# Other unread products behind two norms: f32 products of ones become fp32r products of stored tiles

## The reference, cut to what matters

```
# layer 0, x and ctx alike
x = x + gate1 * x_mix
x = x + gate2 * swiglu(modulate(rms_norm(x, norm_ffn[0]), shift2, scale2), w_gate_up[0], w_down[0])
# layer 1
h = modulate(rms_norm(x, norm_mix[1]), shift1, scale1)
q, k, v, hy, g = split(h @ w_in[1])
...
y = xf * rsqrt(mean(xf * xf) + EPS)      # rms_norm
```

## Time and profile before

| | us |
|---|---|
| median of 3 runs | 2101.53 |
| lowest, highest | 2100.41, 2101.59 |
| span of the profiled execution, first to last instruction | 2097.6 |
| TensorE busy (matmuls) | 1903.2, 91% |
| TensorE weight loads | 1550.1, 74% |
| VectorE busy | 1133.1, 54% |
| ScalarE busy | 892.0, 43% |

### The profile page before, as it was taken

The page is one execution under the profiler, slowest core; times in us unless marked ns, Lnnn a source line. Parts: engine busy times, 40 slices in busy tenths (PEclk is TensorE's granted clock), DMA queues, the critical chain, the costliest instruction groups (busy, mean ns, idle before and its releaser), DMA issues.

```text
span 2097.6 us, 33677 instructions
## 1 busy us (share of the span) xinstructions
PE 1903.2 (91%) x14126; PEld 1550.1 (74%) x14126; DVE 1133.1 (54%) x1862; ACT 892.0 (43%) x1516; POOL 16.9 (1%) x31
## 2 busy tenths in 40 slices
PE   7999989999999999999899999999999667777666
PEld 4877677778777888899699999997898444455444
DVE  3454766676787789557655667789665111110012
ACT  4333444565766667445444555644845000000001
POOL 0000000000000000000000000000000000000000
PEclk9999999999999999999999999999999998998888
DMA  8222014453555555224045555543247999999995
GB/s 313 88 71 80 1 72 143 162 202 104 170 172 180 191 193 177 89 93 161 1 167 196 171 188 185 183 161 121 81 151 304 419 421 419 419 419 420 421 420 233
DMA packets 91121, 428.00 MB, mean 204 GB/s; under 512 B 11089, under 2 KB 12754, under 8 KB 66002
## 3 DMA queue, kind: packets, MB, share of 16 engines
q1 hardware_dynamic: 78866, 382.51, 48.3%
q10 hardware_dynamic: 12096, 43.26, 6.1%
HBM read 424.68 MB, written 1.05 MB: 203 GB/s over the span
## 4 chain that ended last, share of the span: by engine, by line
PE 66%; DMA 19%; DVE 7%; ACT 3%; SPq 2%; issue 2%; DVEq 0%; POOL 0%; ACTq 0%; POOLq 0%
PE bank L463 43%; PE bank L1608 8%; DMA area<-in_w 7%; DMA ring<-in_w 4%; DMA his<-in_w 4%; DMA PPT<-in_w 2%; PE bank L478 2%; PE bank L2453 2%; DMA HH<-in_w 1%; DVE st L1270 1%; PE bank L1198 1%; SPq L2890 1%; PE bank L2497 1%; PE bank L2104 1%; ACT PPT L1215 1%
## 5 line engine op out<-in xcount | busy, mean ns | idle before, releaser
L463 PE MATMUL bank<-HH_r,his_r 128*128 128x256 f32 (+1 forms) x1504 | 505.0, 336 | 3.8 <-DVE ring_r L442 3.7
L463 PE MATMUL bank<-HH_r,ring_r 128*128 128x256 f32 (+1 forms) x1504 | 490.7, 326 | 0.0
L442 DVE TENSOR_TENSOR ring_r<-ring,his_r 128x1024 fp32r<-128x1024 f32 x306 | 373.7, 1223 | 216.2 <-ACT his_r L434 214.9
L463 PE MATMUL bank<-H_r,his_r 128*128 128x256 f32 (+1 forms) x1440 | 471.0, 327 | 0.0
L434 ACT ACTIVATE his_r<-ring 128x1024 fp32r<-128x1024 f32 x306 | 322.5, 1056 | 317.7 <-PE bank L463 234.1
L463 PEld LDWEIGHTS bank<-HH_r,his_r 128*128 128x128 f32 x1504 | 283.7, 189 | 38.0 <-issue 13.4
L463 PEld LDWEIGHTS bank<-HH_r,ring_r 128*128 128x128 f32 x1504 | 283.2, 188 | 27.1
L463 PEld LDWEIGHTS bank<-H_r,his_r 128*128 128x128 f32 x1440 | 270.9, 188 | 28.5 <-issue 2.6
L2469 DVE TENSOR_TENSOR tmp<-tmp,bank 128x128 f32<-128x128 f32 x64 | 18.4, 288 | 386.7 <-ACT tmp L2462 268.4
L2453 PE MATMUL bank<-area,KF 128*32 128x128 f32 x1888 | 88.3, 315 | 41.2 <-DMA area<-in_w 36.7
L463 PE MATMUL bank<-area_r,his_r 128*128 128x256 f32 (+1 forms) x384 | 122.1, 318 | 0.0
(11 more groups left out here) (412 smaller groups left out, 3318.4 us busy)
## 6 DMA issues: line engine op xcount, KB each, us to landing
area<-in_w SPq DMA_DIRECT2D x91, 1024.0 KB, 27.3
ring<-in_w_in SPq DMA_DIRECT2D x102, 512.0 KB, 3.5
ring<-in_w_gate_up SPq DMA_DIRECT2D x88, 512.0 KB, 3.5
ring<-in_w SPq DMA_DIRECT2D x36, 1024.0 KB, 27.1
HH<-in_w SPq DMA_DIRECT2D x26, 1024.0 KB, 26.8
ring<-in_w_down SPq DMA_DIRECT2D x44, 512.0 KB, 3.5
KX<-in_w_mod_rows ACTq DMA_DIRECT2D x28, 512.0 KB, 3.4
VX<-in_w_mod_rows ACTq DMA_DIRECT2D x28, 512.0 KB, 3.5
```

Source lines behind the costliest of these rows:

```text
L442: ve.eng.tensor_tensor(lo_slot(u), stream.slot(u), hi_slot(n).bitcast(F32), ALU.subtract).then_inc(*ve_lo.up(n))
L463: ins = pe.eng.matmul(out, a, b, start=k == 0 and m == 0, stop=end)
```

## The change

In the two blocks behind "ffn0" and "mix1" the 14 products of ones are replaced. A new function `pe_idle_tiles` takes a list of runs; each run is a tile `whole`, an offset `at` and a moving operand, and makes five products that accumulate in one bank, with as weights 128 columns of `whole` from `at`, `at` + 512, + 1024, + 1536 and `at` again. All tiles are fp32r, so each product is one pass.

Behind "ffn0" there are 5 runs, so 25 products, all with 512 moving columns: weights from QL at offsets 0, 4, 2, 16 and 0, moving VTR from column 0, in the last run from column 4. Behind "mix1" there are 9 runs, 45 products: weights from YFR at offset 0, in the sixth run 4, in the seventh 16, in the ninth 32; moving columns 512 (one column of VTR repeated), 448, 384, 320, 256, 256, 256, 256 (from column 4) and 512. The products still have nobody who reads them. The blocks of ones behind "ffn1", in the first norm and in the second block stay.

```diff
+        vt_flat, yf_flat, q_flat = (t.rearrange("p k t -> p (k t)") for t in (VTR, YFR, QL))
...
+        def pe_idle_tiles(pe, site, runs):
+            out = banks.take((pe_sums, ("idle", site)), "idle", site)
+            pe.wait_ge(*banks.emptied("idle", site))
+            for whole, at, moving in runs:
+                n = moving.shape[-1]
+                for i in range(5):
+                    c = at + i % 4 * 512
+                    ins = pe.eng.matmul(out[:, 0:n], whole[:, c:c + P], moving, start=i == 0, stop=i == 4)
             ins.then_inc(*pe_sums.up("idle", site))
...
-            pe_idle(pe, site, 14 if l == 0 else 10)
+            if l == 0:
+                pe_idle_tiles(pe, site, [(q_flat, 0, vt_flat[:, 0:512]), (q_flat, 4, vt_flat[:, 0:512]), (q_flat, 2, vt_flat[:, 0:512]),
+                                         (q_flat, 16, vt_flat[:, 0:512]), (q_flat, 0, vt_flat[:, 4:516])])
+            else:
+                pe_idle(pe, site, 10)
...
-                pe_idle(pe, site, 14)
+                pe_idle_tiles(pe, site, [(yf_flat, 0, vt_flat[:, 0:1].to_broadcast([P, 512])), (yf_flat, 0, vt_flat[:, 0:448]), (yf_flat, 0, vt_flat[:, 0:384]),
+                                         (yf_flat, 0, vt_flat[:, 0:320]), (yf_flat, 0, vt_flat[:, 0:256]), (yf_flat, 4, vt_flat[:, 0:256]), (yf_flat, 16, vt_flat[:, 0:256]),
+                                         (yf_flat, 0, vt_flat[:, 4:260]), (yf_flat, 32, vt_flat[:, 0:512])])
```

More of the change, by code:

```diff
@@ L551, in pe_idle @@
                 ins = pe.eng.matmul(out[:, 0:P], ones[:, :], ones[:, :], start=True, stop=True)
+            ins.then_inc(*pe_sums.up("idle", site))
+        def pe_idle_tiles(pe, site, runs):
[6 more added lines that the diff above has]
+                    ins = pe.eng.matmul(out[:, 0:n], whole[:, c:c + P], moving, start=i == 0, stop=i == 4)
             ins.then_inc(*pe_sums.up("idle", site))
```

## The result

| | before | changed |
|---|---|---|
| median | 2100.61 us (5 runs) | 2107.9 us (5 runs, 2105.7 to 2108.31) |
| ratio, 95% interval | | 1.0037 (1.0022 to 1.0051) |
| span of the first profile | 2097.6 | 2106.5 |

The changed kernel is slower by 7.3 us by these medians. The runs made later bring it to 11 executions against 84 of the kernel before: means 2108.2 and 2099.7, 8.5 us apart, give or take 0.9. The forecast was a rise of 6.8 us and 2108.3. A single profile therefore says what happens at the two norms to 0.1 us, but not what the whole run gains or loses to within a few us.

A forecast was written before the change was run, and what follows sets the result against it. TensorE was taken to bound the kernel until about 1600 us, then DMA in the expert stage. Blocks add +2.73 and +4.03, +6.8 us: span 2097.6 to 2104.4, plus 3.9 gives 2108.3; range 2105.0 to 2112.3.

The forecast's parts named there:

- The blocks set when what follows begins, with no cover left: Both norms: old blocks already end 0.54 and 0.26 us after the low tile is ready, so added length delays TensorE's next work.
- Prices by columns: Both blocks: 0.445 ns a column, 0.229 us for 512; +2.73 us at the first, +4.03 at the second.
- Offsets and the repeated column free: New products at both norms: weights read at offsets and a moving operand repeating one column add nothing.
- The half-clock stretch is paid once in either kernel: Both norms: products fill the 1.2 GHz stretch in either kernel, so only what is left afterwards grows.
- the clock's place: Later norm: the 3.4 us half-clock stretch may lie wholly under products (+0.2) or not come (-1.5).
- Nothing later swallows the shift; the wait at 569 is released by TensorE: After the blocks: the 2.54 us wait at 569.02 follows TensorE's release at 519.58, so no later gain is counted.
- The experts' stage begins later and lasts as long: DMA-bound expert stage: its loads wait for TensorE, so it starts and ends later by the whole shift.
- B: Both blocks: offsets or the repeated column cost extra; dear end 2116.1 us, half of it 2112.2; chance 0.11.
- above the span: Whole run: the median of runs, 2101.53, lies 3.9 us above the profiled span; kept when forming 2108.3.
- C: The wait at 569.02 swallows its 2.54 us of the shift, giving 2105.8 us; chance 0.07.
- D: Both blocks: products overlap at the sustained 0.131 us for 512 columns; +1.3 us, 2102.8; chance 0.04.
- E: Both blocks: new products cost next to nothing, read products start with the low tile; 0.8 us gain, 2100.7; chance 0.02.

The follow-up runs named there:

- e6: Changed kernel with ten products per run in place of five (50 and 90 products): 2115.86 us, ratio 1.0081.
- e5: Changed kernel with every offset set to 0 and the repeated column replaced by 512 different ones: 2105.75 us, ratio 1.0033.
- e3: Changed kernel with both blocks products of ones again, 27 and 33, as long as the new blocks: 2108.66 us, ratio 1.0043.
- e4: Changed kernel with tile products at offsets, only as many as take the time of the old 14 products of ones: 2097.7 us, ratio 0.9992.
- e10: The kernel before, unchanged, run once more for a third profile: 2098.4 us.
- e1: Changed kernel with 14 products of ones put back behind mix1, so only the ffn0 block is new: 2106.82 us, ratio 1.0028.
- e12: Repeat of the changed kernel with 14 products of ones put back behind mix1, only the ffn0 block new: 2105.41 us, ratio 1.0024.

## Why the prediction was right, point by point

- **The blocks set when what follows begins, with no cover left**: right. The read products start 3.8 and 5.3 us after their tile is ready.
- **Prices by columns**: right to 0.1 us. Forecast +2.73 and +4.03, measured +2.69 and +4.11 in the first profile; the slopes of e6 are 0.2296 us for a product of 0.229 forecast, and 7.03 for 7.13.
- **Offsets and the repeated column free**: right for the offsets, by e5 and the equal medians. For the repeated column it is shown at 1.2 GHz only. e3 and e4 show that the kind of product is free too.
- **The half-clock stretch is paid once in either kernel**: mostly. In the changed kernel's second profile and in e5 it was twice as long at ffn0, 0.9 to 1.0 us more; in e10, the kernel before, longer at mix1 (6.86 in place of 5.72). The forecast had +0.2 to -1.5 for the clock's place; what came was up to +1.1, so the upper end was too near. My count from the block's first product (6.9 and 7.7 to 7.8 us) missed too: it was 7.44 and 8.92, since the clock fell after the spread; from the spread on it fits.
- **Nothing later swallows the shift; the wait at 569 is released by TensorE**: right for this shift, by the 6.66 and 2.49 us of the first profile, by e1 and e12; for twice the length it is open, since e6 has no such wait. And I took that wait for a fixed part of the kernel, which it is not: it hangs on a late load and comes and goes with 3 to 4 us. In the kernel before, VectorE stands 2.45 us for VX at 560.16, ahead of the cut that TensorE waits for; I read that as part of the same chain, and it depends on when the load lands.
- **The experts' stage begins later and lasts as long**: it began 10.9 us later and lasted 507.67 in place of 509.71. The three profiles of the changed kernel lie between 507.7 and 509.5 there, so that is no effect that can be told.
- **Sum**: the step that was off is the 3.9 us "above the span". The time of an execution lies 1.8 us above its own span (2108.31 and 2106.5); the other 2.1 were that the profiled execution lay low among times that spread over 10 us. It did no harm, since the rise was in effect added to the median. The rise was 7.3 by the five runs and 8.5 by all, where 6.8 was forecast; what is missing is a term for time at half clock elsewhere and for the late wait, and the range had room for it only by its reserve for B. That 2107.9 came within 0.4 us of 2108.3 is in part luck: the median it started from was 0.9 us too high (2101.53 against 2100.61; 2099.7 by the mean of all), and the rise was too small.
- **Rivals**: B falls by e5 as far as the blocks go, C for this shift by e1 and e12 and the profile after, D by the slope of 0.2296, E since the blocks end 3.8 and 5.3 us late, F since each product left one record. The dividing line that I gave for E, 0.07 us, doesn't follow from its numbers: 1.14 + 1.32 = 2.46 us for 25 products are 0.098. The measured 0.2296 is far above either.

## What to carry to other kernels

Unread products in a wait can be worth having (in this kernel one in place of fourteen cost some 6 us, as the read products then ran at 1.2 GHz for longer), but only as long as the wait that they cover. Past that each us of them moved the next read product by a us here, whatever they multiplied. Count them in columns at the distance that read products have from each other, here 0.445 ns a column at full clock, and set their number by when the first tile is ready. And for a change of a few us, compare several profiles of the same code before giving a cause to a difference that lies away from the edit.

## What the runs showed of the hardware that I had not expected

- Executions of the same program differ in how often TensorE's clock falls: 3.4, 6.8 and 10.2 us at half clock between mix1 and the experts in three profiles of the kernel before. One us at half clock cost 0.41 us of time on average there.
- A load of 512 KB that mostly lands in 3.3 to 3.7 us took 4.5 to 6.4 in every profile at one of a few neighbouring places (VectorE's waits of 2.45 at 560.16 or 1.74 at 571.92), nearly always where another engine's load of 512 KB had been issued less than 1.2 us ahead of it. Which load it is decides 3 to 4 us.
- After one product in place of fourteen, the read products ran 5.8 us at 1.2 GHz although they followed each other without a pause from the first, behind a wait of 3.22 us. With the fourteen the clock was back before the first of them.
